# Three changes joined in a two-layer encoder: a reordered start, four modulation groups summed on VectorE, and an output that is turned and stored in two halves

## The chip, the core and the metric

The kernel runs on one core of a Trainium2 chip. The metric is the device time of one execution in microseconds (us), lower being better. TensorE (PE in the rows) multiplies, VectorE (DVE), ScalarE (ACT) and GpSimd (POOL) work on elements, and the SyncE queue (SP) issues most transfers.

## The reference

Two layers of an encoder work on 320 token rows (256 of a prompt, 64 of a running stream) of width 1024. Each layer is a SwiGLU half step, a token mixer (retention and differential attention) and a second SwiGLU half step. Every one of these three parts is modulated by nine vectors per layer, computed from a conditioning vector c:

```python
mod = (jax.nn.silu(c) @ w_ada[l] + b_ada[l]).reshape(B, N_SUB, 3, D_MODEL)[:, :, :, None, :]
def pre(t, i):
    return _rms_norm(t, g_norm[l, i]) * (1.0 + mod[:, i, 1]) + mod[:, i, 0]
x = x + 0.5 * mod[:, 0, 2] * _swiglu(pre(x, 0), w_ff_up[l, 0], w_ff_down[l, 0])
x = x + mod[:, 1, 2] * mix
x = x + 0.5 * mod[:, 2, 2] * _swiglu(pre(x, 2), w_ff_up[l, 1], w_ff_down[l, 1])
```

All inputs and outputs are float32. `w_ada` alone holds 2 x 9 matrices of 1024 x 1024, 4 MB each.

## The kernel before

**Feed-forward steps.** The activations stay in `x`, with 128 features on the partitions, 8 blocks `kb` and 320 token columns. A feed-forward part, `ffn(l, f, s0)` on every engine, has 22 up steps and 8 down steps, so there are four of them: (0, 0), (0, 1), (1, 0) and (1, 1). For each step the SP queue loads 1 MB of weights (two halves) into `raw`, ACT copies them rounded into `w_hi`, and DVE and POOL compute the rest `w_lo` (the `split` functions). PE then multiplies every block three times (`three`: high by high, high by low, low by high). The weight buffers are double, so the split of step i+2 is done in DVE's iteration i, behind `gate_up(i)`, which evacuates PE's result of step i. In an up step POOL computes the last 512 columns of `w_lo`, and then `g_lo`. Everything is ordered by semaphores and by the order written out by hand for each engine.

**Modulation.** The 18 modulation vectors are "groups". A group is a 1024 x 1024 matrix, loaded in 8 "units" of 512 KB. `ada_pair(b)` multiplies two units, 8 matmuls each of which shows as two records in the trace, into one PSUM bank (two rows, one for each conditioning vector). When a group is complete ACT copies the rows (`copy_rows`), PE turns them into columns (`select`), and DVE adds the bias (`take`). The first two groups are done before the first feed-forward part. The others are placed as pairs between the two halves of up and down steps, by the table that `ada_steps` makes. `ada_slot` and `ada_land` name the buffer and the semaphore of a unit in a ring of six.

**Start.** The SP queue issues the constants, four small loads of biases and gains, x, and then 16 units, with the weights of step 0 after unit 7 and those of step 1 after unit 11. PE turns x and multiplies the units as they land. ACT and DVE scale x to `h_hi` and `h_lo` (`scale_head`, `scale_tail`), and `shift_columns` puts the shift behind the tokens as two more columns. `stay_busy` is a run of 15 matmuls whose result is not used (30 records), and stands right ahead of the first step.

**End.** After the last down step PE turns all of x back (24 transposes, one for each token tile and block), ACT copies three tiles of 1024 columns, and POOL issues three stores.

Of the kernel before, what the change touches and what calls it, by code (L numbers as in the profile page):

```python
# [67 lines left out]
ADA_GROUPS = [(0, 0), (0, 1)] + [(0, k) for k in range(2, 9)] + [(1, k) for k in range(9)]  # L68
# [6 lines left out]

def ada_steps(l, f):


    groups = FFN_GROUPS[l, f]
    pairs = list(range(groups[0] * 4, groups[-1] * 4 + 4))  # L80
    late = LAST_PAIRS if f == 0 else 0
    steps = {b: 2 + i // 2 * 2 * (24 if late else 26) // max(len(pairs) - late, 20)
             for i, b in enumerate(pairs[:len(pairs) - late])}
    steps.update({b: UP + DOWN for b in pairs[len(pairs) - late:]})
    return steps
# [6 lines left out]
def selects_at(l, f, i):  # L92

    return [b // 4 for b, step in ada_steps(l, f).items() if b % 4 == 3 and step + 2 == i]


def copies_at(l, f, i):
    return [b // 4 for b, step in ada_steps(l, f).items() if b % 4 == 3 and step == i]
# [77 lines left out]
def encoder(nc, x_prompt, x_sample, cache_k, cache_v, state_ret, c_prompt, c_sample, w_ada, b_ada, g_norm,  # L176
# [17 lines left out]
    with ExitStack() as ctx:  # L194
# [11 lines left out]
        x = sb("x", [P, KB, TOK])  # L206
        h_hi = sb("h_hi", [P, KB, TOKS], F32R)
# [3 lines left out]
        ones = sb("ones", [P, P])  # L211
        c_rows = sb("c_rows", [16, P])
# [46 lines left out]
        x_nat = arena[:, 0:3 * D].rearrange("p (t d) -> p t d", t=3)  # L259
        q_nat, k_nat, v_nat = region(3, 512), region(3, 512), region(3, 512)  # L260
# [26 lines left out]
        k_dec = tail(5, "k_dec", [P, 3, 256])  # L287
        probs_t = nc.alloc_sbuf_tensor_at("probs_t", [P, 2, 5 * P], F32, offset=tf_at)
# [13 lines left out]
        ada_used = sem("ada_used")  # L302
        acc_cleared = sem("acc_cleared")
# [57 lines left out]
        y_turned, y_copied = sem("y_turned"), sem("y_copied")  # L361
# [8 lines left out]
        def ada_slot(n):  # L370

            if n < RING or n >= 8 * FIRST_GROUPS:
                return ada_raw[n % RING]
            return first_raw[n - RING]

        def ada_land(n):

            if n < RING:
                return ada_landed[n], 16
            if n < 8 * FIRST_GROUPS:  # L380
                return first_landed[n - RING], 16
            again = n // RING - (8 * FIRST_GROUPS - 1 - n % RING) // RING
            return ada_landed[n % RING], 16 + 16 * again
# [45 lines left out]
        SCORE_BANK, TURN_BANK, OWN_BANK = 3, 5, 7  # L429
        RET_BANK = (0, 1, 2)  # L430
# [34 lines left out]
        def _(sp):  # L465
# [3 lines left out]
            for l in range(DEPTH):  # L469
                sp.dma_start(param_rows[0:72, l, :], b_ada[l].rearrange("(r p) -> r p", p=P)).then_inc(bias_landed, 16)  # L470
                sp.dma_start(param_rows[72:96, l, :], g_norm[l].rearrange("s (k p) -> (s k) p", p=P)).then_inc(bias_landed, 16)
# [31 lines left out]
            def load_unit(n):  # L503

                if n >= 8 * FIRST_GROUPS:
                    before = n - RING if n - RING >= 8 * FIRST_GROUPS else n % RING
# [65 lines left out]


        @block.tensor
        def _(pe):
# [58 lines left out]

            def select(group):
# [8 lines left out]

            def ada_between(l, f, i):

                for group in selects_at(l, f, i):
                    select(group)
                for b in pairs_at(l, f, i):
                    ada_pair(b)  # L650
# [55 lines left out]
            def ffn(l, f, s0):  # L706
# [6 lines left out]
                if f == 0:  # L713
# [5 lines left out]
                    for _ in range(6):  # L719
                        pe.matmul(ps[:, 3, 0:P], ones[:], ident, start=True, stop=True)  # L720
# [295 lines left out]
            for b in range(4):  # L1016
                ada_pair(b)
            pe.wait_ge(ones_ready, 1)
            sum_squares(0, 2)
            for b in range(4, 6):  # L1020
                ada_pair(b)
            pe.wait_ge(bias_ready, 1)
            select(0)
            for b in range(6, 8):
                ada_pair(b)
            select(1)
            wait_apart(pe, mod_taken, 2)
            stay_busy()
# [25 lines left out]
            pe.wait_ge(x_ready, KB + DEPTH * 3 * KB)  # L1054
            for t in range(3):
                for half in range(2):
                    for b in range(4):
                        mm = pe.transpose(ps[0:ROWS[t], 2 * t + half, b * P:(b + 1) * P],
                                          x[:, 4 * half + b, TILE0[t]:TILE0[t] + ROWS[t]], ident)
                mm.then_inc(y_turned, 1)  # L1060
# [3 lines left out]
        def _(act):  # L1064
# [45 lines left out]
            std_of(0)  # L1110
            copy_rows(0)
            split(0, 0)
            split(0, 1)
            copy_rows(1)
# [52 lines left out]

            def ffn(l, f, s0):
# [10 lines left out]
                for m in range(DOWN):  # L1179
# [789 lines left out]
```

## Time and profile before

| | us |
|---|---|
| median of 3 runs (1387.49 to 1387.98) | 1387.97 |
| the profiled execution's own time | 1387.66 |
| its span, from the first to the last instruction | 1385.9 |
| PE busy in the span | 1349.5 |
| DVE, ACT, POOL busy | 855.8, 571.2, 406.5 |

The profiled execution is 1.76 us longer than its span, and 0.31 us below the median. Busy times of PE count pipelined matmuls. A few records can be missing.

### The profile page before, as it was taken

Reading aid. Unit: us, or ns where it says so; the run is one execution under the profiler, and the core shown is the slowest. Engines: PE = TensorE matmul, PEld = TensorE weight load, DVE = VectorE, ACT = ScalarE, POOL = GpSimd, SP = SyncE. Lnnn points to the kernel's source line nnn. Section 1 sums busy time; section 2 is a strip of 40 time slices with the busy share of each in tenths; the row PEclk is TensorE's granted clock in tenths of the full one; section 3 lists DMA queues with packets and bytes.
Section 4 is the critical chain, followed back from the end, with each engine's and each line's share of the span. In section 5 each row is a group of like instructions: output and inputs, shape, how many; then the busy total and the mean of one; then the engine's idle time right before and its main releaser. Section 6 shows DMA issues by size and latency. Waiting matters only on the chain.

```text
span 1385.9 us, 23955 instructions
## 1 busy us (share of the span) xinstructions
PE 1349.5 (97%) x9641; PEld 1225.6 (88%) x9641; DVE 855.8 (62%) x1370; ACT 571.2 (41%) x974; POOL 406.5 (29%) x288
## 2 busy tenths in 40 slices
PE   4999999999999999999999999999999999999998
PEld 2799999996778999999999999999676799999997
DVE  1567556548766955556666765655587686666652
ACT  3434334234554643334334433433454553444431
POOL 1133333321202333334323333343021133333431
PEclk9899999999999999999999999999999999999999
DMA  9787778735523687676558678665344257455661
GB/s 310 271 264 218 238 247 255 212 108 159 183 96 100 185 272 235 209 255 168 155 174 259 211 230 256 191 184 188 106 158 143 92 154 244 128 152 153 170 165 38
DMA packets 322813, 261.14 MB, mean 188 GB/s; under 512 B 8256, under 2 KB 288400, under 8 KB 322576
## 3 DMA queue, kind: packets, MB, share of 16 engines
q1 hardware_dynamic: 321248, 255.15, 60.1%
q0 software_dynamic: 1456, 4.46, 0.9%
q8 instruction: 77, 1.26, 0.4%
q14 instruction: 32, 0.26, 0.1%
HBM read 255.12 MB, written 4.46 MB: 187 GB/s over the span
## 4 chain that ended last, share of the span: by engine, by line
PE 92%; SPq 2%; DVE 2%; DMA 2%; POOL 1%; DVEq 0%; issue 0%; ACT 0%; ACTq 0%
PE ps L605 23%; PE ps L607 23%; PE ps L606 23%; PE ps L631 4%; PE ps L801 3%; PE ps L764 3%; PE ps L806 3%; PE ps L802 3%; SPq L509 1%; DMA arena<-in_cache_k 1%; SPq L488 1%; PE ps L731 1%; PE ps L827 1%; PE ps L684 1%; PE ps L683 1%; PE ps L688 1%
## 5 line engine op out<-in xcount | busy, mean ns | idle before, releaser
L1375 DVE TENSOR_TENSOR w_lo<-raw,w_hi 128x1024 fp32r<-128x1024 f32 (+3 forms) x304 | 477.5, 1611 | 69.3 <-ACT w_hi L1084 68.1
L605 PE MATMUL ps<-h_hi,w_hi 128*128 128x322 f32 x1344 | 420.6, 313 | 0.0
L607 PE MATMUL ps<-h_hi,w_lo 128*128 128x322 f32 x1344 | 417.2, 310 | 0.0
L606 PE MATMUL ps<-h_lo,w_hi 128*128 128x322 f32 x1344 | 416.5, 310 | 0.0
L1084 ACT ACTIVATE w_hi<-raw 128x1024 fp32r<-128x1024 f32 (+1 forms) x304 | 324.4, 1115 | 202.9 <-PE ps L607 185.0
L1870 POOL TENSOR_TENSOR w_lo<-raw,w_hi 128x512 fp32r<-128x512 f32 (+1 forms) x112 | 209.4, 1870 | 631.8 <-ACT w_hi L1084 631.8
L605 PEld LDWEIGHTS ps<-h_hi,w_hi 128*128 128x128 f32 x1344 | 253.4, 189 | 12.2 <-issue 12.2
L606 PEld LDWEIGHTS ps<-h_lo,w_hi 128*128 128x128 f32 x1344 | 254.3, 189 | 0.0
L607 PEld LDWEIGHTS ps<-h_hi,w_lo 128*128 128x128 f32 x1344 | 252.6, 188 | 0.0
L1151 ACT ACTIVATE t_buf<-t_buf,shift_w 128x256 f32<-128x256 f32 (+1 forms) x176 | 65.9, 421 | 405.7 <-DVE t_buf L1453 405.7
L605 PE MATMUL ps<-g_hi,w_hi 128*128 128x320 f32 x704 | 217.7, 309 | 0.0
L607 PE MATMUL ps<-g_hi,w_lo 128*128 128x320 f32 x704 | 217.4, 309 | 0.0
L606 PE MATMUL ps<-g_lo,w_hi 128*128 128x320 f32 x704 | 217.4, 309 | 0.0
L605 PEld LDWEIGHTS ps<-g_hi,w_hi 128*128 128x128 f32 x704 | 132.4, 188 | 0.9 <-issue 0.9
L1452 DVE COPY shift_w<-ps 128x4 f32<-128x4 f32 x88 | 14.2, 162 | 192.3 <-PE ps L607 185.3
L606 PEld LDWEIGHTS ps<-g_lo,w_hi 128*128 128x128 f32 x704 | 132.4, 188 | 0.0
L607 PEld LDWEIGHTS ps<-g_hi,w_lo 128*128 128x128 f32 x704 | 132.4, 188 | 0.0
L1875 POOL TENSOR_TENSOR g_lo<-f_buf,g_hi 128x320 fp32r<-128x320 f32 x88 | 113.3, 1288 | 0.0
L1468 DVE SCALAR_TENSOR_TENSOR x<-ps,mod,x 128x256 f32<-128x256 f32 x96 | 31.6, 377 | 126.9 <-PE ps L607 126.9
L1907 POOL TENSOR_TENSOR small<-small,minus_half 128x4 f32<-128x4 f32 (+2 forms) x24 | 35.4, 1481 | 233.0 <-DVE small L1539 129.0
L801 PE MATMUL ps<-w_hi,h_hi 128*128 128x512 f32 x192 | 82.8, 431 | 2.8 <-ACT h_sample L1126 2.4
L1458 DVE SCALAR_TENSOR_TENSOR f_buf<-f_buf,shift_w,t_buf 128x256 f32<-128x256 f32 (+1 forms) x176 | 60.1, 382 | 36.8 <-ACT t_buf L1151 36.8
(184 smaller groups left out, 1475.4 us busy)
## 6 DMA issues: line engine op xcount, KB each, us to landing
raw<-in_w_ff_up SPq DMA_DIRECT2D x176, 512.0 KB, 5.3
ada_raw<-in_w_ada SPq DMA_DIRECT2D x134, 512.0 KB, 6.7
raw<-in_w_ff_down SPq DMA_DIRECT2D x64, 704.0 KB, 6.6
raw<-in_w_in SPq DMA_DIRECT2D x48, 512.0 KB, 4.1
raw<-in_w_out SPq DMA_DIRECT2D x16, 512.0 KB, 4.2
first_raw<-in_w_ada SPq DMA_DIRECT2D x10, 512.0 KB, 8.1
out<-arena POOLq DMA_DIRECT2D x9, 256.0 KB, 4.0
arena<-in_cache_k SPq DMA_DIRECT2D x2, 1024.0 KB, 6.8
```

The source lines that it names most:

```text
L605: pe.matmul(out, hi, mhi, start=start, stop=False)
L606: pe.matmul(out, hi, mlo, start=False, stop=False)
L607: return pe.matmul(out, lo, mhi, start=False, stop=stop)
L631: mm = pe.matmul(ps[32 * j:32 * j + 2, 4 + group % 2, 0:256], groups_c[:, :, k], ada_slot(n)[:, 256 * j:256 * j + 256], start=(k == 0), st ...
L764: mm = pe.matmul(ps[a * DEC:(a + 1) * DEC, 5 if cb == 1 else 2, 0:256], h_sample[:, 4 * kh + k, :], raw[s % 2][:, o:o + 256], start=(kh == ...
L801: pe.matmul(ps[:, first + t, :], tok, wh, start=(k == 0), stop=False)
L1084: act.activation(w_hi[s % 2][:, hf * w:(hf + 1) * w], raw[s % 2][:, hf * w:(hf + 1) * w], ACT.Copy).then_inc(hi_ready, 1)
L1151: last = act.activation(t_buf[:, s % 2, a:b], t_buf[:, s % 2, a:b], ACT.Silu, bias=shift_w[:, s % 2, 0, g:g + 1])
L1375: dve.tensor_tensor(w_lo[s % 2][:, cols], raw[s % 2][:, cols], w_hi[s % 2][:, cols], ALU.subtract)\
L1458: last = dve.scalar_tensor_tensor(f_buf[:, u, a:b], f_buf[:, u, a:b], shift_w[:, u, 1, g:g + 1], t_buf[:, u, a:b], ALU.add, ALU.mult)
L1870: pool.tensor_tensor(w_lo[s % 2][:, cols], raw[s % 2][:, cols], w_hi[s % 2][:, cols], ALU.subtract)\
L1875: pool.tensor_tensor(block_of(g_lo, i + 2 * j), f_buf[:, i % 2, :], block_of(g_hi, i + 2 * j), ALU.subtract)\
```

## The change

**Start.** The order of the first two groups is turned round: group 0 is now the scale (kind 1), group 1 the shift (kind 0). Bias and gain loads go behind unit 1, and the weights of step 1 behind unit 15. ACT and DVE scale x as soon as group 0 has been taken, ahead of the norm's square root. PE selects group 0 ahead of the sum of squares, and unused matmuls stand in packets of 6 (12 records) behind each of the last four pairs and behind `select(1)`, in place of 15 in one run.

**Sums on VectorE.** Groups 5, 11, 15 and 17, one for each feed-forward part, are no longer multiplied unit by unit on PE. They are loaded in 16 half units of 256 KB, one in each of the steps 3 to 18. In its iterations 1 to 16 DVE multiplies a half unit by one column of silu(c), for both conditioning vectors, and adds it to accumulators of 128 x 512 (two instructions for each half unit). In step 18 PE sums the accumulators over the partitions with 8 matmuls (16 records) by a matrix `pick` of ones and zeros. The other groups' pairs are placed anew: those ahead of the summed group at steps 2, 4, 6, 9, 11 and 13, two pairs each.

**End.** Blocks 0 to 3 of x are turned within the last part's down step 6 (12 transposes), copied by ACT and stored. Behind the last down step PE turns blocks 4 to 6 without a wait for block 7, then block 7 in three transposes. ACT copies tiles 0 and 2, DVE tile 1, of 512 columns each, and the SP queue issues the stores.

```diff
-ADA_GROUPS = [(0, 0), (0, 1)] + [(0, k) for k in range(2, 9)] + [(1, k) for k in range(9)]
+ADA_GROUPS = [(0, 1), (0, 0)] + [(0, k) for k in range(2, 9)] + [(1, k) for k in range(9)]
...
+SUM_GROUP = {(0, 0): 5, (0, 1): 11, (1, 0): 15, (1, 1): 17}
+SUM_STEP = 18
+HALF_UNITS = 2 * KB
...
+    groups, own = FFN_GROUPS[l, f], SUM_GROUP[l, f]
+    ahead = [b for g in groups if g < own for b in range(4 * g, 4 * g + 4)]
+    behind = [b for g in groups if g > own for b in range(4 * g, 4 * g + 4)]
+    places = (len(ahead) + 1) // 2
+    steps = {b: 2 + 14 * (i // 2) // places for i, b in enumerate(ahead)}
...
+            def load_half_unit(l, f, k):
+
+                before = (l * 2 + f) * HALF_UNITS + k - 2
+                if before >= 0:
+                    sp.wait_ge(half_used, before + 1)
+                layer, kind = ADA_GROUPS[SUM_GROUP[l, f]]
+                o = kind * D + k % 2 * 512
+                sp.dma_start(half_raw[k % 2][:], ada_d[layer, :, k // 2, o:o + 512]).then_inc(half_landed[k % 2], 16)
...
+                    if 3 <= i < 3 + HALF_UNITS:
+                        load_half_unit(l, f, i - 3)
...
-                if n in (7, 11):
-                    load(0, S_UP1 + n // 11, 0, up_parts(0, 0, n // 11))
+                if n in (7, 15):
+                    load(0, S_UP1 + n // 15, 0, up_parts(0, 0, n // 15))
...
+            def ada_sums(l, f):
+
+                group = SUM_GROUP[l, f]
+                wait_apart(pe, rows_copied, group - 1)
+                if l == 0 and f == 0:
+                    wait_apart(pe, pick_ready, 1)
+                wait_apart(pe, half_used, (l * 2 + f + 1) * HALF_UNITS)
+                for g in range(2):
+                    for j in range(4):
+                        mm = pe.matmul(ps[32 * j:32 * j + 2, 4 + group % 2, 0:256], pick[:, g, :],
+                                       ada_acc[g][j // 2][:, 256 * (j % 2):256 * (j % 2) + 256], start=(g == 0), stop=(g == 1))
+                mm.then_inc(ada_used, 8)
...
+            def turn_y(half):
+
+                n = KB + (DEPTH * 3 - 1) * KB
+                for t in range(3):
+                    for b in range(4):
+                        kb = 4 * half + b
+                        if half == 1 and kb == KB - 1:
+                            continue
+                        if t == 0:
+                            wait_apart(pe, x_ready, n + kb + 1)
+                        mm = pe.transpose(ps[0:ROWS[t], Y_BANK[half][t], b * P:(b + 1) * P],
+                                          x[:, kb, TILE0[t]:TILE0[t] + ROWS[t]], ident)
...
+            def add_half_unit(l, f, k):
+
+                kb, hf = divmod(k, 2)
+                dve.wait_ge(half_landed[hf], 16 * ((l * 2 + f) * KB + kb + 1))
+                for g in range(2):
+                    acc, c = ada_acc[g][hf][:], silu_c[:, g * KB + kb:g * KB + kb + 1]
+                    if kb == 0:
+                        last = dve.tensor_scalar(acc, half_raw[hf][:], c, None, ALU.mult)
+                    else:
+                        last = dve.scalar_tensor_tensor(acc, half_raw[hf][:], c, acc, ALU.mult, ALU.add)
+                last.then_inc(half_used, 1)
...
                 for i in range(UP):
                     gate_up(l, s0 + i, 0, f, i)
                     split(l, s0 + i + 2)
+                    if 1 <= i < 1 + HALF_UNITS:
+                        add_half_unit(l, f, i - 1)
...
+            dve.wait_ge(y_turned, 5)
+            dve.tensor_copy(y_nat[:, 1, 512:D], ps[:, Y_BANK[1][1], :]).then_inc(y_middle, 1)
...
-                store(dst, x_nat[0:ROWS[t], t, :], y_landed)
-            pool.wait_ge(y_landed, 48)
+            pool.wait_ge(y_landed, 96)
```

PE's order at the start, from unit 7 (`first_raw_64`) to the first matmul of step 0, stood so before (L590 and L593 are the sum of squares, L641 `select`, L602 `stay_busy`, L683 step 0):

```order
L631 MATMUL ps<-first_raw_64,silu_c 2x256 x4
L590 MATMUL ps<-std,ones 128x320
L593 MATMUL ps<-t_buf,ones 128x320 x2
...
L641 MATMUL ps<-tab,ada_rows 128x8 x2
...
L631 MATMUL ps<-first_raw_72,silu_c 2x256 x4
L641 MATMUL ps<-tab,ada_rows 128x8 x2
L602 MATMUL ps<-tab,ones 128x128 x15
L683 MATMUL ps<-h_hi,w_hi 128x322
```

In the changed kernel the same stretch reads (L706 is `select`, L643 and L646 the sum of squares, L654 `stay_busy`, L772 step 0):

```order
L683 MATMUL ps<-first_raw_64,silu_c 2x256 x4
L706 MATMUL ps<-tab,ada_rows 128x8 x2
L643 MATMUL ps<-std,ones 128x320
L646 MATMUL ps<-t_buf,ones 128x320 x2
...
L683 MATMUL ps<-first_raw_72,silu_c 2x256 x4
L654 MATMUL ps<-tab,ones 128x128 x6
L706 MATMUL ps<-tab,ada_rows 128x8 x2
L654 MATMUL ps<-tab,ones 128x128 x6
L772 MATMUL ps<-h_hi,w_hi 128x322
```

So the first `select` moved up behind unit 7, and a packet of 6 unused matmuls now stands on either side of the second one.

One DVE iteration of an up step of the last feed-forward part now reads as follows (L1555 to L1561 are `gate_up`, L1466 `split`, L1478 `add_half_unit`):

```order
L1555 COPY shift_w<-ps 128x4
L1556 TENSOR_TENSOR t_buf<-ps,rstd 128x320
L1557 TENSOR_TENSOR f_buf<-ps,rstd 128x320
L1561 SCALAR_TENSOR_TENSOR f_buf<-f_buf,shift_w,t_buf 128x256
L1561 SCALAR_TENSOR_TENSOR f_buf<-f_buf,shift_w,t_buf 128x64
L1466 TENSOR_TENSOR w_lo<-raw,w_hi 128x1024
L1466 TENSOR_TENSOR w_lo<-raw,w_hi 128x512
L1478 SCALAR_TENSOR_TENSOR ada_acc_88<-half_raw_86,silu_c,ada_acc_88 128x512
L1478 SCALAR_TENSOR_TENSOR ada_acc_90<-half_raw_86,silu_c,ada_acc_90 128x512
```

The last two rows are new. They stand behind the split and ahead of the next `gate_up`.

## Rows read from the trace of the kernel before

**Rows 1.** The page: span, and shares of the chain that ended last.

```profile
span 1385.9 us, 23955 instructions
...
PE 92%; SPq 2%; DVE 2%; DMA 2%; POOL 1%; DVEq 0%; issue 0%; ACT 0%; ACTq 0%
```

**Rows 2.** The chain that ended last, at the start: start us, us, what.

```profile
39.71 1.08 PE ps L631 x8
...
41.49 1.00 PE ps L641 x4
...
42.84 5.33 PE ps L602 x30
```

**Rows 3.** Timeline of the start: start us, us, engine, line, operation, tiles.

```profile
1.94 0.30 SPq L470 DMA_DIRECT2D param_rows<-in_b_ada  x1
...
3.52 0.84 SPq L474 DMA_DIRECT2D arena<-in_x_prompt  x2
...
30.99 1.04 PE L631 MATMUL ps<-first_raw,silu_c 128*2 128x256 f32 x8 [0.31 <-DMA first_raw<-in_w_ada]
...
35.83 1.03 PE L631 MATMUL ps<-first_raw,silu_c 128*2 128x256 f32 x8 [2.85 <-DMA first_raw<-in_w_ada]
...
43.03 5.22 ACT L1133 ACTIVATE h_hi<-x,mod 128x256 fp32r<-128x256 f32 x16 [1.83 <-DVEq L1392]
```

**Rows 4.** Windows of the start: busy by engine, granted clock, transfer share, GB/s.

```profile
30.00:36.00 6.00, 2.84 (x24) 1.15 (x20) 2.89 (x4) 1.46 (x2) 0.00 (x0) 0.50 1.11 356
...
56.00:64.00 8.00, 8.00 (x57) 8.00 (x56) 5.03 (x9) 3.90 (x8) 2.66 (x2) 1.00 0.28 80
```

**Rows 5.** PE's groups by line: the same unused matmul elsewhere, at full clock.

```profile
L720 PE MATMUL ps<-tab,ones 128*128 128x128 f32 x24 | 3.2, 284 | 0.0
```

**Rows 6.** DVE's timeline in up steps of the last feed-forward part, pairs within the first.

```profile
1152.18 0.15 DVE L1452 COPY shift_w<-ps 128x4 f32<-128x4 f32 x1
...
1161.31 0.16 DVE L1452 COPY shift_w<-ps 128x4 f32<-128x4 f32 x1 [3.91 <-PE ps L607]
...
1192.25 0.16 DVE L1452 COPY shift_w<-ps 128x4 f32<-128x4 f32 x1 [2.34 <-PE ps L607]
...
1194.57 2.92 DVE L1375 TENSOR_TENSOR w_lo<-raw,w_hi 128x1024 fp32r<-128x1024 f32 x2 [0.26 <-ACT w_hi L1084]
...
1199.36 0.16 DVE L1452 COPY shift_w<-ps 128x4 f32<-128x4 f32 x1 [1.09 <-PE ps L607]
```

**Rows 7.** DVE's and POOL's timelines in one up step of the first part.

```profile
87.84 0.16 DVE L1452 COPY shift_w<-ps 128x4 f32<-128x4 f32 x1 [2.48 <-PE ps L607]
...
93.01 0.90 DVE L1516 SCALAR_TENSOR_TENSOR rope_c<-tab,gqk_rows 128x64 f32<-128x64 f32 x1
...
92.49 1.33 POOL L1875 TENSOR_TENSOR g_lo<-f_buf,g_hi 128x320 fp32r<-128x320 f32 x1
```

**Rows 8.** Groups by line and shape: operation, shapes, count, busy us, mean ns.

```profile
L1766 DVE SCALAR_TENSOR_TENSOR arena<-arena,unit_s 128x576 f32<-128x576 f32 x4 | 3.3, 818 | 0.3
L1375 DVE TENSOR_TENSOR w_lo<-raw,w_hi 128x1024 fp32r<-128x1024 f32 x160 | 195.4, 1240 | 45.6 <-ACT w_hi L1084 44.4
L1375 DVE TENSOR_TENSOR w_lo<-raw,w_hi 128x128 fp32r<-128x128 f32 x32 | 97.4, 3043 | 0.0
```

**Rows 9.** Timeline of the end.

```profile
1376.30 0.68 DVE L1468 SCALAR_TENSOR_TENSOR x<-ps,mod,x 128x256 f32<-128x256 f32 x2 [9.00 <-PE ps L607]
...
1377.03 2.84 PE L1058 MATMUL ps<-tab,x 128*128 128x128 f32 x24 [0.77 <-DVE x L1468]
1378.16 2.83 ACT L1352 ACTIVATE arena<-ps 128x1024 f32<-128x1024 f32 x3 [18.51 <-PE ps L1058]
...
1381.28 0.53 POOL L1910 DMA_DIRECT2D out<-arena  x1 [0.33 <-ACT arena L1352]
```

**Rows 10.** ACT's group of half-bank copies, and POOL's stores of the whole kernel.

```profile
L1200 ACT ACTIVATE arena<-ps 128x512 f32<-128x512 f32 x20 | 12.0, 602 | 23.0 <-PE ps L731 23.0
...
DMA to landing us min/median/max: 2.2/3.7/4.4
```

More of the change, by code:

```diff
@@ L73 @@
 LAST_PAIRS = 3
+SUM_GROUP = {(0, 0): 5, (0, 1): 11, (1, 0): 15, (1, 1): 17}
+SUM_STEP = 18
+HALF_UNITS = 2 * KB
 def ada_steps(l, f):
-    groups = FFN_GROUPS[l, f]
-    pairs = list(range(groups[0] * 4, groups[-1] * 4 + 4))
+    groups, own = FFN_GROUPS[l, f], SUM_GROUP[l, f]
[3 more added lines that the diff above has]
+    steps = {b: 2 + 14 * (i // 2) // places for i, b in enumerate(ahead)}
     late = LAST_PAIRS if f == 0 else 0
-    steps = {b: 2 + i // 2 * 2 * (24 if late else 26) // max(len(pairs) - late, 20)
-             for i, b in enumerate(pairs[:len(pairs) - late])}
-    steps.update({b: UP + DOWN for b in pairs[len(pairs) - late:]})
+    steps.update({b: 20 + i // 2 * 2 for i, b in enumerate(behind[:len(behind) - late])})
+    steps.update({b: UP + DOWN for b in behind[len(behind) - late:]})
     return steps
@@ L92, in selects_at, with ring_place, unit_at @@
 def selects_at(l, f, i):
-    return [b // 4 for b, step in ada_steps(l, f).items() if b % 4 == 3 and step + 2 == i]
+    return [b // 4 for b, step in ada_steps(l, f).items() if b % 4 == 3 and step + 2 == i] + \
+        ([SUM_GROUP[l, f]] if i == SUM_STEP + 2 else [])
 def copies_at(l, f, i):
-    return [b // 4 for b, step in ada_steps(l, f).items() if b % 4 == 3 and step == i]
+    return [b // 4 for b, step in ada_steps(l, f).items() if b % 4 == 3 and step == i] + \
+        ([SUM_GROUP[l, f]] if i == SUM_STEP else [])
+def ring_place(n):
+    return n - 8 * sum(g < n // 8 for g in SUM_GROUP.values())
+def unit_at(place):
+    return [n for n in range(8 * len(ADA_GROUPS)) if n // 8 not in SUM_GROUP.values()][place]
 RQK, RV, RG, DQ, DK, DVAL = range(6)
@@ L211, in encoder @@
         ones = sb("ones", [P, P])
+        pick = sb("pick", [P, 2, 2])
         c_rows = sb("c_rows", [16, P])
@@ L302, in encoder @@
         ada_used = sem("ada_used")
+        half_landed = [sem(f"half_landed{s}") for s in range(2)]
+        half_used, pick_ready = sem("half_used"), sem("pick_ready")
         acc_cleared = sem("acc_cleared")
@@ L505, in load_unit @@
                 if n >= 8 * FIRST_GROUPS:
-                    before = n - RING if n - RING >= 8 * FIRST_GROUPS else n % RING
+                    place = ring_place(n)
+                    before = unit_at(place - RING) if place - RING >= 8 * FIRST_GROUPS else place % RING
                     sp.wait_ge(ada_used, before + 1)
@@ L571, in _ @@
                 load_ffn(l, 1, S_UP2)
+            for half in range(2):
+                cols = slice(512 * half, 512 * half + 512)
+                for t in range(3) if half == 0 else (0, 1, 2):
+                    if half and t == 1:
+                        sp.wait_ge(y_middle, 1)
+                    else:
+                        sp.wait_ge(y_copied, 3 * half + t + 1 - (half and t == 2))
+                    dst = y_prompt[0, t * P:(t + 1) * P, cols] if t < 2 else y_sample[0][:, cols]
+                    sp.dma_start(dst, y_nat[0:ROWS[t], t, cols]).then_inc(y_landed, 16)
         @block.tensor
@@ L718, in ffn @@
                     ada_pair(late[2])
-                    for _ in range(6):
-                        pe.matmul(ps[:, 3, 0:P], ones[:], ident, start=True, stop=True)
+                    stay_busy(6)
                 else:
@@ L1051, in _ @@
                 ffn(l, 1, S_UP2)
[L1054 to L1060, printed above, removed]
+            turn_y(1)
         @block.scalar
@@ L1166, in tail_blocks, with copy_y @@
                     square_down(l, f, m)
+            def copy_y(half, tiles):
+                for t in tiles:
+                    act.wait_ge(y_turned, 3 * half + t + 1)
+                    act.activation(y_nat[0:ROWS[t], t, 512 * half:512 * half + 512], ps[0:ROWS[t], Y_BANK[half][t], :], ACT.Copy)\
+                        .then_inc(y_copied, 1)
             def ffn(l, f, s0):
@@ L1348, in _ @@
                 ffn(l, 1, S_UP2)
[L1350 to L1353 removed]
+            copy_y(1, (0, 2))
         @block.vector
@@ L1566, in _ @@
             dve.drain()
-            rstd_of(0)
             take(0)
-            split(0, 0)
-            split(0, 1)
-            take(1)
             dve.sem_inc(mod_scaled, 1)
@@ L1574, in _ @@
                 if l == 0:
-                    shift_columns(0)
                     for kb in range(KB):
                         scale_tail(0, kb)
+                    split(0, 0)
+                    rstd_of(0)
+                    take(1)
+                    shift_columns(0)
+                    split(0, 1)
                 else:
```

77 lines of the change are left out of this document (48 added, 29 removed).

## The prediction

> **What bounds the kernel now.** I read the page first. The span is 1385.9 us, and PE holds 92% of the chain that ended last [rows 1]. So a change is worth what it takes off PE's own queue, or off the two ends where PE waits. Next came the chain at the start: PE gets the last of its 16 units at 39.71, and the chain then runs through the second `select` and 5.33 us of unused matmuls to 48.17 (42.84 + 5.33), where step 0 begins [rows 2]. The timeline of the start shows what the units wait for: unit 11 is multiplied at 30.99, unit 12 at 35.83, although three units later take only 3.88 us (35.83 to 39.71) [rows 2, 3]. The windows show PE at half its clock (0.50, that is 1.2 GHz) from 30 to 36 [rows 4]. Last I read DVE's timeline within the up steps, because DVE gets new work there, and the timeline of the end.
>
> **Term 1, the start.** A unit takes (39.71 - 35.83) / 3 = 1.29 us. Between units 11 and 12 lie 4.84 us, of which 3.55 are the weights of step 1 [rows 2, 3]. These now go behind unit 15, and four small loads that stood from 1.94 to 3.52 on the queue ahead of x go behind unit 1: 1.58 us more [rows 3]. Transfers limit this stretch, so the last unit should be there at 39.71 - 3.55 - 1.58 = 34.6.
>
> Behind it now stand on PE: 8 records of the unit, 12 unused records, `select`, and 12 unused records. At the full clock an unused record takes 3.2 / 24 = 0.133 us [rows 5], so 12 take 1.6. The unit took 1.08 and `select` 1.00 at half the clock [rows 2]; at full I take half of each. Sum: 0.55 + 1.6 + 0.5 + 1.6, and 0.2 for the gaps, = 4.5. Step 0 begins at 39.1 in place of 48.2: **-9.0 us**. Scaling x took 5.22 us behind the second group [rows 3]; it now follows the first group, with some 10 us to spare. DVE's `take` and `shift_columns` (about 0.8 us from `select` to the shift) are covered by the last 1.6 us of unused matmuls. At half the clock the 24 records take 24 x 5.33 / 30 = 4.3, the rest twice the above, with the gaps 6.5 in all: step 0 at 41.1. If the earlier pairs and packets are slow too (2.1 + 2.1 for each pair against 2.6 of landing), three of them add 4.8 more, and the gain falls to 2. That is the far bound. A little more than forecast, -10.5, is the other one.
>
> Do the next weights keep up? Those of step 1 land near 34.6 + 3.55 = 38.2, and step 0 covers their split until about 46. All that is queued by then has landed before where the transfer share falls, at about 57 (0.28 in the window 56 to 64) [rows 4]. The queue runs 1.6 us ahead of before, so now at about 55. Its last part, the weights of step 3, is wanted by ACT at 39.1 + 7.1 + 7.1 + 1.3 = 54.6, and needed by PE a step later. A wait of half a microsecond is hidden.
>
> **Term 2, the pairs.** An up step of the last part takes 7.11 us (1192.25 to 1199.36) and one with two pairs 9.13 (1152.18 to 1161.31) [rows 6]: 1.01 for a pair, its gaps included. Four groups of four pairs go: -16.2. Each `ada_sums` has 16 records of a pair's shapes, so it costs 1.01 too: +4.0. The selects and the bytes loaded stay. PE's sum is **-12.2 us**.
>
> This holds if DVE's new work stays hidden. Its iteration before ends with the split at 1194.57 + 2.92 = 1197.49, that is 5.24 after 1192.25, so 1.87 of 7.11 is idle [rows 6]. No row shows a multiply-add of 512 columns; 576 columns take 818 ns [rows 8], so I take 0.75 each. The first of the two also meets POOL. In the first part's steps a small operation of the same kind stands in this place: it starts at 93.01, takes 0.90, and ends at 93.91, just behind POOL's `g_lo` (92.49 + 1.33 = 93.82) [rows 7]. It waited for POOL. So the first multiply-add ends about 6.07 + 448 columns x 1.05 ns = 6.55 after the iteration's start (93.91 - 87.84 = 6.07), the second at 7.25. That is 0.14 us longer than a step without pairs, and far shorter than one with them. In the last part no pairs are left, so DVE falls behind by 0.14 in each of 16 iterations, 2.2 us in all. The first half of a split ends 1194.57 + 1.24 - 1192.25 = 3.6 after the iteration's start [rows 6, 8], and PE needs it at 7.1, so 3.5 us of lag cost nothing. I take 0. In the other parts the steps with pairs give DVE 2 us each back, six times. Bounds: 1.45 of new time (no wait for POOL), no cost; 2.4, a lag of 0.53 in each of 16 iterations, 8.5 - 3.5 = 5 us in the last part.
>
> The Trainium skill speaks against this place for the work: its page "SBUF — State Buffer" (section "SBUF: two separate sides") says that VectorE with two SBUF inputs and GpSimd hold a shared port pair by an exclusive lock, for the whole instruction. The trace agrees: DVE's 128-column part of a split, run against POOL, takes 3043 ns where 1024 columns take 1240 [rows 8]. By that rule each multiply-add can wait for a whole POOL instruction, which is the third rival below.
>
> The SP queue: a half unit's load waits for DVE's iteration before, about 2 us after the weights' own wait is over, and its landing has most of a step to spare. Loads of pairs behind it already wait longer than that for PE. 0.
>
> **Term 3, the end.** Before, from DVE's last update at 1376.30 to the end of the span are 9.6 us: 24 transposes of 2.84 in all, ACT's three copies to 1380.99, the last store at 1381.28, and 4.6 from its issue to the end [rows 1, 9]. Now PE turns blocks 4 to 6 while DVE updates block 7 (9 x 0.118 = 1.1, about 1376.2 to 1377.3), then block 7 (to 1377.7). Two copies of 0.60 on ACT [rows 10] end near 1378.7, with DVE's third beside them. The SP queue issues at about 0.45 each, the last at 1379.1. No row shows a store from this queue: POOL's stores landed in 2.2 to 4.4, median 3.7 [rows 10]; I take 3.0, since the tiles are half as large. With some 0.6 behind the landing, the end is at 1382.7: -3.2. The first half's 12 transposes now stand in down step 6 on PE: 12 x 0.118, with gaps +1.5. ACT has nothing else there. Sum **-1.7 us**; with 2.2 and 4.4 it is -2.5 and -0.3.
>
> **Sum.** -9.0 - 12.2 - 1.7 = -22.9. The profiled execution took 1387.66, so 1364.8; the median of the runs lies 0.31 higher: **1365 us**.
>
> **Rivals.**
> - *The start gives less.* PE stays or falls back to half its clock between the packets, or the units do not come earlier. For it: the clock was at 0.50 from 30 to 36, with PE busy for 2.84 of 6 us [rows 4]. Against it: the packets fill most of these gaps. 2 to 7 us are lost: 1367 to 1372.
> - *DVE runs over its slack in the last part*, by the 2.4 bound: up to +5, 1366 to 1370.
> - *DVE becomes the bound in all four parts, and the kernel is slower.* The 16 steps last on average 7.96 us in the first three parts (12 pairs of 1.01 and three selects of about 0.5, half of the 1.00 at half the clock) and 7.11 in the last. DVE's iteration is 5.24 + e, and about 0.4 more in the parts of each layer's first half, an estimate for the small work that stands there [rows 7], 0.1 in (0, 1). Past 3.5 us of lag PE waits: 64e - 146 - 14 us in all. This eats 23 us at e = 2.86 in place of my 2.0. It would take both multiply-adds waiting for POOL, 0.8 more; by the rows only one POOL instruction stands there. At e = 3.1 PE loses 38 us, and the kernel takes about 1403.
> - *The end saves nothing*, since a store costs as before: +1.5, 1366.5.
>
> **How the numbers follow.** The forecast has 0.57 (1362.5 to 1366.5), the weaker start 0.20, the last part's lag 0.10, the end 0.08, slower 0.03. That the sums do nothing at all is 0.02: it would need PE not to be the bound, against 92% of the chain, and gives 1377. The range 1361 to 1370.5 leaves out the far third of the weak start and the two last cases, and on the low side a start of more than 10 us with a cheap store. About 0.2% (2.8 us) is what the runs here can tell from no change. Faster 0.95, same 0.02, slower 0.03.
>
> **What would show it.** Term 1: the last unit at 34 to 36, granted clock 1.00 throughout, step 0 at 38.5 to 40.5. Term 2: steps of 7.1 in the last part from step 2 to 17, multiply-adds of 0.75, the first of them longer by its wait, and no idle time of PE ahead of `w_lo`. Term 3: an end of about 6.4 us behind the last update, and a down step 6 that is 1.5 longer than its neighbours. The forecast is wrong if PE waits for DVE in the up steps, if the clock falls ahead of step 0, or if the weights of steps 2 and 3 land after PE wants them.

## The result and the profile after

The changed kernel takes **1366.14 us** (median of 4 runs, 1363.97 to 1367.47) against 1387.97 for the kernel before: a ratio of 0.9842 with a 95% interval of 0.9825 to 0.9859. Forecast were 1365 and 1361 to 1370.5. The profiled execution took 1366.7 us, 1.8 more than its span. All medians here are of undisturbed executions; one of `u_end` (below) took 2315.26 us, at a mean granted clock of 0.70, and is left out.

This is the page of the changed kernel (as [rows 1]): span, busy times and chain.

```profile
span 1364.9 us, 23813 instructions
...
PE 1339.9 (98%) x9479; PEld 1224.7 (90%) x9479; DVE 964.2 (71%) x1502; ACT 571.3 (42%) x976; POOL 405.2 (30%) x285
...
PE 94%; DVE 2%; DMA 2%; SPq 1%; POOL 1%; DVEq 0%; issue 0%; ACT 0%; ACTq 0%
```

PE still holds the chain. DVE gained 108 us of work, and PE lost 10. The next is the changed kernel's chain at the start (as [rows 2]: start us, us, what).

```profile
26.07 0.61 PE ps L683 x8
26.68 2.86 PE ps L654 x12
29.54 1.22 PE ps L683 x16
...
34.81 0.98 PE ps L683 x16
35.79 1.53 PE ps L654 x12
37.32 0.35 PE ps L706 x4
37.67 1.44 PE ps L654 x12
39.11 0.15 PE ps L772
```

Step 0 (L772) begins at 39.11, before at 48.17. But from unit 9 (26.07) on the chain is PE alone: units (L683) and packets (L654) follow each other with no wait for a transfer. The last unit had landed at 34.64 by the trace, ahead of the last 16 records' start (34.81). The windows (as [rows 4]: PE, PEld, DVE, ACT and POOL busy, granted clock, transfer share, GB/s) say why: PE was at half its clock for some 3 us.

```profile
26.00:28.00 2.00, 1.93 (x14) 1.50 (x15) 2.00 (x7) 2.00 (x7) 0.00 (x0) 0.65 1.03 408
28.00:30.00 2.00, 2.00 (x16) 1.50 (x18) 1.74 (x4) 1.98 (x3) 0.00 (x0) 0.50 1.02 406
30.00:32.00 2.00, 2.00 (x27) 1.41 (x17) 1.57 (x2) 1.32 (x2) 0.00 (x0) 0.99 1.04 414
```

Timeline of POOL and DVE in up steps of the last part (as [rows 6, 7]; L1982 is `g_lo`, L1478 are the two multiply-adds, L1466 the split, L1555 opens the next iteration):

```profile
1212.48 1.33 POOL L1982 TENSOR_TENSOR g_lo<-f_buf,g_hi 128x320 fp32r<-128x320 f32 x1
...
1213.00 2.02 DVE L1478 SCALAR_TENSOR_TENSOR ada_acc<-half_raw,silu_c,ada_acc 128x512 f32<-128x512 f32 x2
1214.94 0.15 DVE L1555 COPY shift_w<-ps 128x4 f32<-128x4 f32 x1
...
1217.26 2.92 DVE L1466 TENSOR_TENSOR w_lo<-raw,w_hi 128x1024 fp32r<-128x1024 f32 x2 [0.27 <-ACT w_hi L1164]
1220.10 2.02 DVE L1478 SCALAR_TENSOR_TENSOR ada_acc<-half_raw,silu_c,ada_acc 128x512 f32<-128x512 f32 x2
1222.05 0.16 DVE L1555 COPY shift_w<-ps 128x4 f32<-128x4 f32 x1
```

The iteration takes 1222.05 - 1214.94 = 7.11 us. The wait for PE of 1.09 to 2.34 ahead of the copy [rows 6] is gone: the multiply-adds fill it, and DVE's iteration has just the length of PE's step. All multiply-adds of the kernel (duration in ns: min, median, max; first and last start):

```profile
L1478 DVE SCALAR_TENSOR_TENSOR ada_acc<-half_raw,silu_c,ada_acc x112: 735/1048/1369, 74.8 to 1249.8; 128x512 f32<-128x512 f32 x112
```

The median lies between two groups: the 56 that come first in their pair start within POOL's `g_lo` and take 1.352 to 1.369 us, the 56 that come second meet no POOL instruction and take 0.735 to 0.743.

Timeline of the end (as [rows 9]; L720 and L727 turn the second half, L624 are the stores from the SP queue):

```profile
1359.23 1.14 PE L720 MATMUL ps<-tab,x 128*128 128x128 f32 x9
1359.43 0.68 DVE L1571 SCALAR_TENSOR_TENSOR x<-ps,mod,x 128x256 f32<-128x256 f32 x2 [9.01 <-PE ps L659]
1360.25 0.52 PE L727 MATMUL ps<-tab,x 128*128 128x128 f32 x3
1360.59 1.07 ACT L1248 ACTIVATE y_nat<-ps 128x512 f32<-128x512 f32 x2 [15.00 <-PE ps L727]
...
1361.21 1.34 SPq L624 DMA_DIRECT2D out<-y_nat  x3
```

The issues of line L624 by themselves (as [rows 10]; first and last start in us):

```profile
L624 SPq DMA_DIRECT2D out<-y_nat x6: 338/396/498, 1344.7 to 1362.1; - x6
...
DMA to landing us min/median/max: 2.0/2.3/2.4
```

PE turns nine blocks while DVE still updates the last one, and the end lasts 1364.9 - 1359.43 = 5.47 us in place of 9.6.

The stages between DVE's marks (its first copy of each part and its updates of x) put the difference in its places, in us:

| stage | before | after | difference | forecast |
|---|---|---|---|---|
| to the end of step 0's matmuls | 55.32 | 46.25 | -9.07 | -9.0 |
| up steps, four parts | 180.90, 175.09, 176.07, 161.53 | 177.97, 172.17, 173.12, 158.74 | -2.93, -2.92, -2.95, -2.79 | -3.03 each |
| attention of layer 0, of layer 1 | 145.25, 145.45 | 145.16, 148.07 | -0.09, +2.62 | 0, 0 |
| last part's down steps | 67.76 | 69.08 | +1.32 | +1.5 |
| end | 9.60 | 5.47 | -4.13 | -3.2 |

All other stages agree within 0.03. The sum is -20.94; the spans differ by 21.0. The attention of layer 1, which nobody touched, gives back 2.6 us. It loses them where PE waits for the cached keys (a row of PE's timeline, then windows, columns as above):

```profile
987.76 0.66 PE L819 MATMUL ps<-tab,arena 128*128 128x128 f32 x4 [2.07 <-DMA arena<-in_cache_k]
```

```profile
986.00:988.00 2.00, 0.24 (x2) 0.24 (x3) 1.89 (x2) 1.30 (x3) 0.00 (x0) 1.00 0.99 376
988.00:990.00 2.00, 2.00 (x10) 1.67 (x9) 1.85 (x5) 0.60 (x1) 0.00 (x0) 0.79 0.09 33
990.00:992.00 2.00, 2.00 (x6) 1.55 (x5) 1.93 (x3) 0.00 (x0) 0.00 (x0) 0.50 0.00 0
```

PE stood still for 2.07 us (1.07 before), and then the granted clock fell to 0.50.

### The profile page after: what moved, and what is told of

Its sections match the earlier page's. It is cut to its first block, busy times and chain, and to the rows that moved or that the text cites. A ratio compares the mean times of both kernels' runs of the same rounds, so it can differ in the third digit from the quotient of the medians.

```text
span 1364.9 us, 23813 instructions
## 1 busy us (share of the span) xinstructions
PE 1339.9 (98%) x9479; PEld 1224.7 (90%) x9479; DVE 964.2 (71%) x1502; ACT 571.3 (42%) x976; POOL 405.2 (30%) x285
## 4 chain that ended last, share of the span: by engine, by line
PE 94%; DVE 2%; DMA 2%; SPq 1%; POOL 1%; DVEq 0%; issue 0%; ACT 0%; ACTq 0%
PE ps L657 24%; PE ps L659 23%; PE ps L658 23%; PE ps L683 3%; PE ps L889 3%; PE ps L852 3%; PE ps L894 3%; PE ps L890 3%; DMA arena<-in_cache_k 1%; PE ps L819 1%; PE ps L915 1%; PE ps L773 1%; PE ps L772 1%; PE ps L777 1%; PE ps L654 1%; SPq L514 1%
## 5 line engine op out<-in xcount | busy, mean ns | idle before, releaser
L1466 DVE TENSOR_TENSOR w_lo<-raw,w_hi 128x1024 fp32r<-128x1024 f32 (+3 forms) x304 | 477.7, 1612 | 74.5 <-ACT w_hi L1164 73.5
L1982 POOL TENSOR_TENSOR g_lo<-f_buf,g_hi 128x320 fp32r<-128x320 f32 x88 | 113.5, 1289 | 0.0
L1478 DVE SCALAR_TENSOR_TENSOR ada_acc<-half_raw,silu_c,ada_acc 128x512 f32<-128x512 f32 x112 | 113.3, 1050 | 0.0
L1561 DVE SCALAR_TENSOR_TENSOR f_buf<-f_buf,shift_w,t_buf 128x256 f32<-128x256 f32 (+1 forms) x176 | 60.0, 382 | 36.9 <-ACT t_buf L1228 36.9
```

The costliest lines, as they stand in the source:

```text
L1466: dve.tensor_tensor(w_lo[s % 2][:, cols], raw[s % 2][:, cols], w_hi[s % 2][:, cols], ALU.subtract)\
L1478: last = dve.scalar_tensor_tensor(acc, half_raw[hf][:], c, acc, ALU.mult, ALU.add)
L1561: last = dve.scalar_tensor_tensor(f_buf[:, u, a:b], f_buf[:, u, a:b], shift_w[:, u, 1, g:g + 1], t_buf[:, u, a:b], ALU.add, ALU.mult)
L1982: pool.tensor_tensor(block_of(g_lo, i + 2 * j), f_buf[:, i % 2, :], block_of(g_hi, i + 2 * j), ALU.subtract)\
```

## The experiments

**Theory:** the three terms are real, add up, and are of the forecast sizes; the attention of layer 1 is lost to a late load and the clock behind it. **Rivals:** the gain of a part comes with another part of the change (an interaction); DVE's added work already costs something; the start is bound by PE's clock and packets, not by transfers. Times are medians; all ratios are to the kernel before on the same chip.

**One part undone at a time.** `u_start` puts the old start back:

```diff
-ADA_GROUPS = [(0, 1), (0, 0)]
+ADA_GROUPS = [(0, 0), (0, 1)]
-                if n in (7, 15):
-                    load(0, S_UP1 + n // 15, 0, up_parts(0, 0, n // 15))
+                if n in (7, 11):
+                    load(0, S_UP1 + n // 11, 0, up_parts(0, 0, n // 11))
...
+            select(1)
+            stay_busy(15)
```

> The changed kernel with its start put back as before (order of groups 0 and 1, loads, splits, one run of 15 unused matmuls); the sums and the end stay. If the start is worth what its place shows (step 0 began at 48.17 before and at 39.11 after), this is 9.1 us slower than the changed kernel, about 1375, and step 0 begins at 48. If part of it was given back later, because weights of steps 1 to 3 land too late for the earlier steps, it costs less than 7.

1372.79 us, ratio 0.9891 (0.9878 to 0.9905). Its chain at the start is that of before again:

```profile
31.27 7.97 DMA first_raw<-in_w_ada
...
39.29 1.08 PE ps L681 x8
...
42.42 5.10 PE ps L652 x30
```

Step 0 begins at 47.52, 8.4 later than in the changed kernel's profile. The time is 6.65 above that median, 8.3 above the one taken again (below): the attention of layer 1 took 145.21 here, so the loss of 2.6 was absent.

`u_sums` multiplies groups 5, 11, 15 and 17 on PE again, with all pairs placed as before:

```diff
-                    if 1 <= i < 1 + HALF_UNITS:
-                        add_half_unit(l, f, i - 1)
...
+SUM_GROUP = {}
```

> The changed kernel with all 18 groups multiplied on TensorE again and no sums on VectorE; start and end stay. By the four feed-forward parts (2.9, 2.9, 2.95 and 2.8 us shorter after the change) this should be 11.6 us slower, about 1377.5. The rival: the new DVE work or its loads also cause the longer wait for the cached keys in layer 1 (2.6 us in the profiled execution); then only about 9 come back, and this kernel's runs lie as close together as those of before (0.6 us).

1375.04 us, ratio 0.9910 (0.9896 to 0.9923). The up steps of the four parts take 180.90, 175.06, 176.03 and 161.53 us: those of before to 0.04. That is 2.93, 2.89, 2.91 and 2.79 more, 11.5 in all; the median moved by 8.9 against the first set and 10.6 against the second. Its rival, that the sums make the keys of layer 1 late, has PE's wait of 0.17 for it and the runs against it: they spread over 2.5 us, not 0.6.

`u_end` turns and stores the output as before, behind the last step:

```diff
-                if (l, f, i) == (DEPTH - 1, 1, UP + 6):
-                    turn_y(0)
...
+                pool.wait_ge(y_copied, t + 1)
+                store(dst, x_nat[0:ROWS[t], t, :], y_landed)
```

> The changed kernel with the end put back: all of x turned after the last step, three copies of 1024 columns on ACT, three stores from POOL. By the places (the end 4.1 us shorter, down step 6 1.3 longer) this should be 2.8 us slower, about 1369. The rival that the end saves nothing: the same time within 0.5 us.

1368.91 us (median of 3), ratio 0.9861 (0.9845 to 0.9876). Its end takes 9.49 us (4.02 more) and the last down steps 67.76 (1.32 less): 2.7 in all, against 2.8 and 4.5 by the medians. Its attention of layer 1 again took 147.91, with a wait of 1.91 for the keys.

By stage the three effects sum to 8.4 + 11.5 + 2.7 = 22.6 us. The change as a whole has 9.07 + 11.59 + 4.13 - 1.32 = 23.5 without the attention's loss; the 0.9 between them is less than what the start varies by from run to run (next). So no interaction of the parts shows that is larger than this.

**The changed kernel once more**, without an edit, beside the next four.

> The changed kernel itself once more, beside the next three on the same chip. Theory: its runs spread over some 3.5 us because TensorE's clock falls, or does not, at two waits: between the units of the start, and at the keys of layer 1. Then the profile shows all other stretches as in the first one (feed-forward parts within 0.1 us), and the time goes with the mean clock of the run: 1364 at 1.00, 1367 at 0.996.

1364.46 us (1363.5 to 1366.02), ratio 0.9829 (0.9815 to 0.9842). PE waited 0.67 for the keys of layer 1, and that attention took 145.10. Unit 9 was multiplied only at 27.43, the clock was 0.50 until 32, and step 0 began at 41.34:

```profile
27.43 1.03 PE ps L683 x8
...
41.34 0.15 PE ps L772
```

Five more profiles have this start without an edit (`u_sums`, `u_end` and, below, `dve_extra`, `cache_split`, `fill`). In the seven, step 0's matmuls end at 45.49 to 48.89, before at 55.32: the start gains 6.4 to 9.8 us, and the table's 9.07 is one draw. The three slowest (47.61 to 48.89) are those in which PE gets unit 9 at 27.39 to 27.71, in place of 25.50 to 26.55: from there PE works without a pause, so the delay is never made up. The expected link with the mean granted clock is loose: 1366.02 us at 0.996, 1364.67 at 0.997, 1363.5 at 0.999, 1364.25 at 1.000. So the start and the attention each vary by 2 us or more between executions. What makes unit 9 or the keys late in some of them stays open.

**DVE's slack.** `dve_extra` adds a third operation of the same size to each of the 64 iterations; its result is not used, since the half unit is loaded anew.

```diff
+                last = dve.scalar_tensor_tensor(half_raw[hf][:], half_raw[hf][:], c, half_raw[hf][:], ALU.mult, ALU.add)
                 last.then_inc(half_used, 1)
```

> One more multiply-add of 512 columns behind each half unit (on the half unit itself, so its result is not used): 0.67 us more in each of 16 iterations of each part. By the lag of the prediction (3.5 us of lag cost nothing, more costs in full) PE loses 16 x 0.67 - 3.5 = 7.2 us in the last part, which has no pairs, and 0 to 1 in the others: about 1373.5. Rival 1: DVE's work is never waited for in these steps: 1366. Rival 2: there is no slack, since the iteration of the last part is now 7.10 and a step is 7.11: 10.7 in the last part, and 2 to 3 in each of the others, 1384.

1372.35 us, ratio 0.9885 (0.9871 to 0.9898). The last part took 165.05 (6.3 more); the other three within 0.1 of the changed kernel's. DVE's timeline there, and the waits of PE from 1190 to 1350 us (total, times, longest):

```profile
1137.32 0.15 DVE L1556 COPY shift_w<-ps 128x4 f32<-128x4 f32 x1
...
1144.55 0.15 DVE L1556 COPY shift_w<-ps 128x4 f32<-128x4 f32 x1
...
1242.39 2.02 DVE L1478 SCALAR_TENSOR_TENSOR ada_acc<-half_raw,silu_c,ada_acc 128x512 f32<-128x512 f32 x2
1244.34 0.74 DVE L1479 SCALAR_TENSOR_TENSOR half_raw<-half_raw,silu_c 128x512 f32<-128x512 f32 x1
1245.00 0.15 DVE L1556 COPY shift_w<-ps 128x4 f32<-128x4 f32 x1
...
1260.54 0.15 DVE L1556 COPY shift_w<-ps 128x4 f32<-128x4 f32 x1
```

```profile
PEld ps L657 <- issue: 6.1, 10, 0.7
...
PE ps L657 <- DVE w_lo L1466: 3.6, 9, 0.4
```

An operation behind the one that waits costs 0.74, and starts at once. Iterations of 1250.16 - 1242.39 = 7.77 us exceed a step by 0.66; the first two, whose multiplies have nothing to add to yet, take 7.23 (1137.32 to 1144.55). All 16 last from 1137.32 to 1260.54, 123.2 us, which is 9.5 more than 16 steps of 7.11, and 6.3 of it reach PE. The slack ahead of the bound is thus 3.2 us, where the forecast had 3.5. In the other parts the steps with pairs give the lag back. The rival that DVE already costs something falls: the changed kernel shows no such wait.

**The start's packets.** `p3` has three unused matmuls behind each pair and four behind the second `select`, in place of six; `p0` has none but six behind the `select`.

```diff
                 ada_pair(b)
-                stay_busy(6)
+                stay_busy(3)
             select(1)
-            stay_busy(6)
+            stay_busy(4)
```

> Packets of 3 unused matmuls behind the last four pairs, in place of 6, and 4 behind the second select. Theory: the packets are what PE waits behind now, since the last two pairs did not wait for their units; so step 0 begins up to 1.5 to 2 us earlier (37.1 to 37.6) if the clock stays at 1.00. Rival: the gaps make the clock fall, and step 0 begins at 39 or later.

> No unused matmuls behind the last four pairs; the 6 behind the second select stay. Theory: as in the kernel before, the clock falls to 0.50 at about 29, and is still there when step 0 begins; the last unit, the select and the packet take twice as long, and the first part of step 0 too, so the end of step 0 comes no earlier than in the changed kernel (46.2), or up to 2 us later. Rival: the packets only delay; step 0 ends 2 us earlier.

`p3`: 1362.75 us, ratio 0.9816 (0.9803 to 0.9830), step 0 at 38.18. `p0`: 1366.49, ratio 0.9840 (0.9826 to 0.9853); its step 0 ends at 47.49, as its theory had it. Windows of `p0`, then its chain: PE waits for nearly every unit, stays at half its clock, and enters step 0 so, at 40.18:

```profile
34.00:36.00 2.00, 1.37 (x12) 0.11 (x8) 0.00 (x0) 0.26 (x1) 0.00 (x0) 0.50 1.17 285
36.00:38.00 2.00, 1.58 (x7) 1.61 (x8) 0.38 (x3) 0.23 (x2) 0.00 (x0) 0.50 0.80 114
38.00:40.00 2.00, 2.00 (x12) 2.00 (x11) 1.16 (x2) 1.98 (x3) 0.00 (x0) 0.50 0.72 99
```

```profile
34.64 1.08 PE ps L683 x8
...
37.42 2.76 PE ps L654 x12
40.18 0.27 PE ps L772
```

By the medians some packets help and six each are too many: `p3` is 1.7 below the changed kernel and `p0` 2.0 above it on the same chip. Both intervals overlap with that of the changed kernel, so this is not shown by the times alone. The profiles speak for it: in `best` (below, with the packets of `p3`) unit 9 came as late as in the slow starts (27.54), and step 0 began at 38.34 all the same. In `p3` the clock was still 0.50 from 28 to 34, so `early` adds five unused matmuls ahead of unit 8, where PE stood still for 1.2 to 1.4 us:

```diff
             sum_squares(0, 2)
+            stay_busy(5)
             for b in range(4, 8):
```

> As with three and four unused matmuls, and with five unused matmuls ahead of unit 8, where PE stood still for 1.4 us. Theory: TensorE is at half its clock from 28 on because it stood still from 23.5 to 26; with the gap filled the granted clock is 1.00 from 24 to 36, PE multiplies each unit as it lands, the last one at about 33.4, and step 0 begins at 33.4 + 0.55 + 0.4 + 0.5 + 1.07 = 35.9 in place of 38.2: 1362.75 - 2.2 = 1360.5 us. Rival: the clock falls all the same, between the units; step 0 at 38.2 or later, and 1363 us.

1363.67 us, ratio 0.9824 (0.9811 to 0.9838). The clock came out as expected, 1.00 in every window from 22 to 36, and the time did not. Its chain at the start:

```profile
22.80 12.12 DMA first_raw<-in_w_ada
...
34.96 0.61 PE ps L683 x8
...
36.91 0.99 PE ps L654 x8
```

The last unit lands at 22.80 + 12.12 = 34.92, not at 33.4 and no earlier than in the changed kernel (34.64): the chain now hangs on the transfers, and step 0 begins at 37.90, 0.3 ahead of `p3`. Units 8 to 15 are multiplied over 10.0 us (24.96 to 34.96) and not 9.0, seven times 1.29, since they do not land evenly: 1.87 lie between units 9 and 10 (26.28 to 28.15). The rate is 404 to 414 GB/s until 32, then 340 and 291. Here the rival won half: with few packets the clock is not what holds the start.

**The wait for the keys.** `cache_split` loads the cached keys in four parts of one tile, and PE waits for each apart:

```diff
-                sp.dma_start(scratch, ck_d[l]).then_inc(cache_landed, 16)
+                for t in range(4):
+                    sp.dma_start(scratch[:, t, :], ck_d[l][:, t, :]).then_inc(cache_landed[t], 16)
...
-                    pe.wait_ge(cache_landed, 16 * l + 16)
+                    pe.wait_ge(cache_landed[n], 16 * l + 16)
```

> The changed kernel with the load of the cached keys cut into four loads of 256 KB with a semaphore each, so that PE's first turn of keys waits for a quarter only. Theory: in layer 1 the changed kernel lost 2.6 us where PE waited 2.07 us for the keys and then ran at half its clock; the wait varies by itself and makes the runs spread. Then the wait goes, the clock stays at 1.00 there, the time is 1362 to 1363.5 and the runs lie within 1 us. Rival: the four pieces land nearly together behind the weights in the queue; then wait and time stay as they are (1364 to 1367.5).

1363.26 us, ratio 0.9825 (0.9812 to 0.9839). The attention of layer 0 took 144.27, that of layer 1 145.36. SP's issues in layer 0 and in layer 1, and a wait of ACT in layer 1:

```profile
316.28 1.82 SPq L602 DMA_DIRECT2D arena<-in_cache_k  x4
...
969.69 8.38 SPq L514 DMA_DIRECT2D raw<-in_w_in  x3
978.19 4.29 SPq L602 DMA_DIRECT2D arena<-in_cache_k  x4
...
983.85 2.01 ACT L1165 ACTIVATE w_hi<-raw 128x1024 fp32r<-128x1024 f32 x2 [3.55 <-DMA raw<-in_w_in]
```

SP spent 4.29 us on the four issues in layer 1 and 1.82 in layer 0. The weights that ACT waits for until 983.85 were issued ahead of them (by 969.69 + 8.38 = 978.07), so they did not stand behind them in the queue, and PE waited 0.51 for the first part of the keys. That four issues hold up the queue is not shown: layer 0, with four, took as long as with two (next).

`best` uses two parts, of one tile and of three, and the packets of `p3` (three behind each pair; the expectation names only the last).

```diff
+                for c, t in enumerate((slice(0, 1), slice(1, 4))):
+                    sp.dma_start(scratch[:, t, :], ck_d[l][:, t, :]).then_inc(cache_landed[c], 16)
...
+                    pe.wait_ge(cache_landed[min(n, 1)], 16 * l + 16)
```

> The changed kernel with three unused matmuls behind the last pair and four behind the second select, and with the cached keys loaded in two parts (one tile, then three) that PE waits for apart. If the wait for the keys is what the attention of both layers loses, each loses it: 144.3 us in layer 0 (145.2 in the changed kernel) and 144.4 in layer 1 (145.1 to 148.1), and step 0 begins at 38.2: 1362.75 - 0.9 - 0.8 = 1361.0 us. Rival: the second part comes as late as the whole did, and PE waits there instead: 1362.7.

**1360.72 us** (1360.27 to 1361.38), ratio 0.9806 (0.9793 to 0.9819). PE waits for no keys at all, and the attention takes 144.23 in both layers, as forecast for this run. `best2` adds the five matmuls of `early`:

> The filled gap ahead of unit 8 and the keys in two parts together. If both theories hold: 1362.75 - 2.2 - 1.7 = 1358.9 us. If only the keys' holds 1361.0; if only the start's 1360.5; if neither 1362.8.

1361.03 us (1360.77 to 1361.35), ratio 0.9808 (0.9795 to 0.9821): the keys' theory alone. In its profile step 0 begins at 37.74, 0.6 ahead of `best`; in the medians nothing of that is left.

`fill` leaves the keys' load whole and puts four unused matmuls ahead of the wait:

```diff
+                    if n == 0:
+                        for _ in range(4):
+                            pe.matmul(ps[:, 6, 0:P], ones[:], ident, start=True, stop=True)
                     pe.wait_ge(cache_landed, 16 * l + 16)
```

> The changed kernel with four unused matmuls (8 records, 1.1 us at the full clock) ahead of PE's wait for the cached keys in each layer. Theory: what layer 1 lost in the profiled run (148.1 us against 145.5) is 1.0 of a later load and 1.6 of a clock that fell because PE stood still for 2.1 us. With the wait filled PE stands still for 1 us at most, the clock stays at 1.00, and the attention of layer 1 takes 145.2 to 146.2 however late the keys are; time 1364.5 to 1365. Rival: the clock falls for another reason, and 0.50 shows behind the keys' wait here too, 147 to 149 us.

1364.19 us, ratio 0.9832 (0.9818 to 0.9845), attention of layer 1 145.70, clock 1.00. This settles nothing: the wait was 0.38 behind 1.1 us of filling, so PE would have stood still for some 1.3 us without it, and at 1.37 (`dve_extra`) no fall shows either. What speaks for the theory are the waits of layer 1 over the runs with the load whole: 0.17, 0.42, 0.67, 0.77, 0.82, 1.07 and 1.37 us gave an attention of 144.63, 144.86, 145.10, 145.21, 145.26, 145.45 and 145.82, so each lost its own wait; 1.91, 2.10 and 2.07 (`u_end`, `early`, the first profile) gave 147.91, 148.04 and 148.07, some 1.5 us more than that. The load of weights issued just ahead of the keys took 5.5 and 5.6 us to land in `u_end` and the first profile, 3.8 to 4.9 in the other runs with the load whole, `early` included. All three long waits are among the nine profiles with sums on DVE and none among the two without (`u_sums` and the kernel before), too few to tell whether the sums' loads play a part. The row of `early`, behind which the window from 988 to 990 shows 0.50:

```profile
986.82 1.12 PE L819 MATMUL ps<-tab,arena 128*128 128x128 f32 x4 [2.10 <-DMA arena<-in_cache_k]
```

## Why the prediction was right

The likeliest case came in: 1366.14 against 1365, all three mechanisms in their places. Step by step:

- **Start, -9.0 forecast, -9.07 measured.** The step "the last unit should be there at 39.71 - 3.55 - 1.58 = 34.6" holds: it landed at 34.64 in the changed kernel's profile, and PE got it at 34.64 to 35.41 where it waited for it (`p0`, `best2`, `early`, `best`). The tail of 4.5 came out as 39.11 - 34.64 = 4.5, though PE was behind and had two units left in it. "Granted clock 1.00 throughout" was wrong: it was 0.50 from 28 to 30, one of the prediction's own signs of being wrong, and until 32 in the second profile, where step 0 came at 41.34. So the close agreement is partly luck: the seven profiles gain 6.4 to 9.8 us. That is the weak start's mechanism (chance 0.20) at its small end, some 2 to 3 us, in some executions. The bound of 41.1, with half the clock behind the last unit, is not tested by any run: `p0` took 40.18 - 34.64 = 5.5 us there at 0.50, with 12 unused records in place of 24, where the bound's prices give 6.5 - 2.1 = 4.4.
- **Pairs and sums, -12.2 forecast, -11.6 measured.** The four pairs less the one sum are -2.79 to -2.95 a part in place of -3.03; the sum's step is 1258.75 - 1250.48 = 8.27 long, 1.16 more than its neighbours and not 1.01, which is the difference. The multiply-add of 512 columns takes 0.735 alone (0.75 taken), the pair 2.02 with its wait (2.0 taken). The first of a pair waits for POOL, as the prediction had it: the longest took 1.369, a wait of 0.63, which lies within the rest of one POOL instruction (`g_lo` ends at 1212.48 + 1.33 = 1213.81, 0.81 behind the pair's start); the second waits for none. By the Trainium skill, page "SBUF — State Buffer", section "SBUF: two separate sides", a VectorE instruction with two SBUF inputs and a GpSimd one that reads SBUF share a port pair, and the one that starts first holds it for the whole instruction; the trace agrees, with 0.63 of waiting behind one instruction. The iteration is 7.11 and not 7.25, so there is no lag to pay for, though no idle time is left either, and the slack is 3.2 and not 3.5.
- **End, -3.2 and +1.5 forecast, -4.13 and +1.32 measured.** The store's landing was the mis-sized term: 3.0 taken, 2.3 measured, near the low bound from POOL's stores. The last issue came 1362.1 - 1359.43 = 2.7 behind the update (2.8 forecast).
- **What the sum left out.** "A wait of half a microsecond is hidden" was argued for the start's weights alone. No term looked at the attention, where the keys' landing sets PE's wait: +2.6 in the first profile, at most 0.4 in the second and in most others, and a part of the spread from 1363.97 to 1367.47. The runs of each of the two kernels with the keys in two parts and smaller packets lie within 1.1 us. Without the attention the places give -23.5, against -22.9 in the sum. Other draws of the start would have given up to 2.6 less, and without the late keys the time would have been some 2.6 lower, so part of the agreement to 1.1 us is luck.

The rival that DVE becomes the bound (slower) is answered by `dve_extra`: the change itself has e = 7.11 - 5.24 = 1.87. A third operation has 7.77 - 5.24 = 2.53, still below the 2.86 from which it decides, and costs 6.3 in the last part and 0.1 or less in each other. The rival's sum over all four parts gives 64 x 2.53 - 146 - 14 = 1.9 there, too little, since the slack of the steps with pairs in the other parts is of no use to the last.

## What to carry to other kernels

Work moved to an engine that is off the critical path is paid by its iteration, not by its busy share: add up the iteration with its waits, set it against the shortest step it must fit into, and carry the excess as a lag until the slack is used. A load that an engine waits for in the middle of a kernel is worth splitting by the first piece it needs: two parts gained about 1 us in each layer, and more where the keys were late. Where a single profile carries the account, take a second one, and look at stages that nobody touched: one late transfer hid a tenth of this gain, and the same start ended 3.4 us apart in seven profiles.

## What the runs showed of the hardware

- With a wait of PE of 1.91 to 2.10 us for the keys the granted clock fell to 0.50 (1.2 GHz); with waits of 0.17 to 1.37 us in the same place it stayed at 1.00. A wait that was 1.0 us longer cost 2.6. That the wait is the cause is argued from these rows; `fill` did not test it.
- A multiply-add of 512 float32 columns on VectorE took 0.735 to 0.743 us alone and 1.352 to 1.369 when it started within a GpSimd instruction.
- Stores of 128 and 256 KB issued from the SP queue landed in 2.0 to 2.4 us, those of POOL before in 2.2 to 4.4.
- Keeping TensorE at its full clock (`early`) gained 0.3 us at the entry to step 0 and nothing in the median, where transfers were the bound; letting it fall (`p0`) cost 2.0 us at that entry against `p3`.
